# Four weight loads of a one-core kernel, each cut into a piece of 120 and a piece of 8 partitions

## What is computed

```
def peer_ffn(h, w_query, sub_keys, expert_u, expert_v):
    q = (ht @ w_query).reshape(T, Hh, 2, PEER_HALF)             # 1024 x 2048 matrix
    scores = einsum('thpd,hpkd->thpk', q, sub_keys)
    s_top, i_top = top_k(scores, 16)
    ...
    best, pos = top_k(cand, 16)                                  # 8 heads x 16 picks a token
    u = expert_u[idx]                                            # rows of 1024 floats
    a = gelu(einsum('tkd,td->tk', u, xb)) * g
    return einsum('tk,tkd->td', a, expert_v[idx])
```

## Time and profile before

| what | value |
|---|---|
| median of 3 runs | 2224.89 us (2223.32 to 2227.02) |
| span of the profiled execution | 2222.0 us |
| that execution's own time | not listed apart; the span is used |
| PE busy | 1963.9 us (88%) |
| DVE busy | 1560.3 us (70%) |
| ACT busy | 1033.6 us (47%) |
| POOL busy | 628.7 us (28%) |
| traffic, mean over the span | 761.24 MB, 343 GB/s |

### The profile page before, as it was taken

How to read it: one execution, slowest core, us unless ns; L and a number is a source line. 1 busy time by engine, 2 the same in 40 slices (tenths; PEclk the granted TensorE clock), 3 DMA queues, 4 the chain that set the end, 5 groups by cost and what they waited for, 6 DMA issues and landing times. The chain is left out here.

```text
span 2222.0 us, 24054 instructions
## 1 busy us (share of the span) xinstructions
PE 1963.9 (88%) x8090; PEld 1240.2 (56%) x8090; DVE 1560.3 (70%) x2943; ACT 1033.6 (47%) x2177; POOL 628.7 (28%) x552
## 2 busy tenths in 40 slices
PE   5999989987777888899999988888898889999998
PEld 5987845432222333479885544343343326888987
DVE  6987877676667775678878876676777755565554
ACT  4345545544444444444445644444455434544443
POOL 1000255544444444000014444444344430200000
PEclk9999999999999999999999999999999999999999
DMA  8897799999999999786589999999999995343553
GB/s 332 296 378 261 312 421 421 420 421 422 421 421 421 421 422 421 291 338 226 206 301 421 414 421 420 421 421 421 421 411 421 421 421 191 115 145 132 189 189 133
DMA packets 112396, 761.24 MB, mean 343 GB/s; under 512 B 12832, under 2 KB 13600, under 8 KB 26128
## 3 DMA queue, kind: packets, MB, share of 16 engines
q0 software_dynamic: 76480, 548.94, 59.7%
q1 hardware_dynamic: 34832, 207.74, 25.2%
q10 hardware_dynamic: 960, 3.01, 0.4%
HBM read 758.60 MB, written 1.05 MB: 342 GB/s over the span
## 5 line engine op out<-in xcount | busy, mean ns | idle before, releaser
L1046 PE MATMUL pair<-uv,p_diag 128*128 128x512 f32 x1352 | 653.2, 619 | 114.3 <-ACT p_diag L2374 112.4
L1743 DVE CUSTOM_DVE_ANT_0 uv<-uv,p_h 128x1024 f32<-128x1024 f32 x338 | 413.7, 1224 | 242.6 <-DMA uv<-in_peer_uv,p_idx 240.7
L573 POOL DMA_INDIRECT uv<-in_peer_uv,p_idx x338 | 398.3, 1179 | 522.8 <-PE pair L1046 385.9
L1046 PEld LDWEIGHTS pair<-uv,p_diag 128*128 128x128 f32 x1352 | 243.8, 193 | 493.5 <-ACT p_diag L2374 271.4
L1314 DVE TENSOR_TENSOR ring_low<-ring,ring_high 128x2048 fp32r<-128x2048 f32 x143 | 326.5, 2297 | 102.6 <-ACT ring_high L2156 101.4
L2366 ACT ACTIVATE p_act<-p_dot 128x1 f32<-128x1 f32 x512 | 103.5, 202 | 627.6 <-DVE p_dot L1743 625.5
L2156 ACT ACTIVATE ring_high<-ring 128x2048 fp32r<-128x2048 f32 x144 | 272.2, 1908 | 187.8 <-DMA ring<-in_ret_w_in 64.5
L725 PE MATMUL pair<-hT_high,ring_high 128*128 128x256 f32 x960 | 287.3, 299 | 0.2
L1046 PE MATMUL pair<-uv_high,p_diag 128*128 128x512 f32 x464 | 229.2, 625 | 52.5 <-ACT p_diag L2374 52.5
L725 PE MATMUL pair<-hT_low,ring_high 128*128 128x256 f32 x960 | 272.1, 283 | 0.0
L725 PE MATMUL pair<-hT_high,ring_low 128*128 128x256 f32 x896 | 254.1, 284 | 0.0
(11 more groups left out here) (413 smaller groups left out, 2660.1 us busy)
## 6 DMA issues: line engine op xcount, KB each, us to landing
ada<-in_ada_w SPq DMA_DIRECT2D x50, 512.0 KB, 5.9
ring<-in_ret_w_in SPq DMA_DIRECT2D x24, 1024.0 KB, 8.2
ring<-in_sgu_w_in SPq DMA_DIRECT2D x24, 1024.0 KB, 6.6
ring<-in_w_up SPq DMA_DIRECT2D x16, 1024.0 KB, 4.8
ring<-in_w_down SPq DMA_DIRECT2D x16, 1024.0 KB, 4.8
mod<-in_ada_w SPq DMA_DIRECT2D x30, 512.0 KB, 5.7
ring<-in_peer_w_query SPq DMA_DIRECT2D x12, 1024.0 KB, 8.5
ring<-in_sgu_w_out SPq DMA_DIRECT2D x12, 1024.0 KB, 4.9
```

What stands on the lines that cost most here:

```text
L573: nc.gpsimd.indirect_dma_start(uv_rows[SLOT[l][s]].rearrange("p a d -> p (a d)"), None, experts, bass.IndirectOffsetOnAxis(ap=p_idx[:, k:k ...
L1046: mm = nc.tensor.matmul(acc[:, half, :], p_diag[:, n % DIAGS, :], v[:, half * 512:(half + 1) * 512], start=(k == 0), stop=(k == PICKS - 1))
L1743: V.tensor_tensor_reduce(out=u, in0=u, in1=p_h[:, s // PICKS, :], scale=1.0, scalar=0.0, op0=ALU.mult, op1=ALU.add, accum_out=p_dot[:, n % ...
```

## The change

Blocks 6 and 7 of each of the two query matrices are no longer loaded by one DMA of 128 partitions but by two: partitions 0 to 119 and partitions 120 to 127, one after the other on SP's queue, into the same slot and with the same semaphore, each raising it by 16. `raw_count` counts two for such a block, so that all later waits on the slot's semaphore are for the matching value.

```diff
--- before.py
+++ after.py
@@ -63,6 +63,7 @@
 MEM_AT = (63, 69)
 MEM_NORM_AT = 22
 TILE_AT = (216, 224)
+MOST = 120
 
 
 TWO_PI_1 = 6.28125
@@ -226,7 +227,8 @@
         raw_at.append(early[i] if i in early else in_ring % R)
         in_ring += i not in early
     raw_before = [max((j for j in range(i) if raw_at[j] == raw_at[i]), default=None) for i in range(limit)]
-    raw_count = [sum(raw_at[j] == raw_at[i] for j in range(i + 1)) for i in range(limit)]
+    in_two = {query_first[l] + e for l in range(2) for e in (6, 7)}
+    raw_count = [sum(1 + (j in in_two) for j in range(i + 1) if raw_at[j] == raw_at[i]) for i in range(limit)]
     high_before = [max((j for j in range(i) if high_at[j] == high_at[i]), default=None) for i in range(limit)]
     low_by_pool = [0]
     low_by_dve = [i for i in range(limit) if i not in low_by_pool]
@@ -531,7 +533,11 @@
                         sp.wait_ge(h_ready, h_count(1 + 2 * l, 1, 1))
                 if i in behind_rows:
                     sp.wait_ge(dot_ready, behind_rows[i])
-                sp.dma_start(raws[raw_at[i]], blocks[i]).then_inc(w_in[raw_at[i]], 16)
+                if i in in_two:
+                    sp.dma_start(raws[raw_at[i]][0:MOST], blocks[i][0:MOST]).then_inc(w_in[raw_at[i]], 16)
+                    sp.dma_start(raws[raw_at[i]][MOST:P], blocks[i][MOST:P]).then_inc(w_in[raw_at[i]], 16)
+                else:
+                    sp.dma_start(raws[raw_at[i]], blocks[i]).then_inc(w_in[raw_at[i]], 16)
                 for j in loaded_after[i]:
                     if j == 6 * KD:
                         sp.wait_ge(x_ready, norm_count(2, 1))
```

## The result

The changed kernel takes 2242.99 us (median of 4 runs, 2241.67 to 2244.02), the kernel before 2224.11 in the runs beside it (2222.38 to 2227.02): ratio 1.0084, 95% interval 1.0072 to 1.0096. It is 18.9 us slower, far outside the range given.

A forecast was written before the change was run, and what follows sets the result against it. The prediction took the picks as bound by the DMA engines, the last to finish deciding. Gains of 1.6 to 2.2 us in layer 0 and 1.8 to 2.4 in layer 1, middle 4.0, gave 2224.9 - 4.0 = 2220.9 us; range 2217.5 to 2227.0.

The forecast's parts named there:

- A row costs 2.49 / 8 = 0.311 us of its engine: Picks and cut loads: a 128-row transfer takes 2.49 us with 8 rows per engine, so each row costs 0.311 us.
- the division that I assumed: Cut loads: 120 rows go to 15 engines, 8 each; the other 8 go to eight engines, 1 each.
- at worst: Cut loads: half of the engines carry the 120 rows, +2.5 us per block and +5.0 us per layer.
- the third: Rival on the cut loads: the 120 rows go to eight engines, the last among them; +5.0 us a layer, 2234.9; chance 0.07.
- the first case: End of each layer's picks: the relieved engine is the last to finish; gain 3.4 to 4.6 us, middle 4.0; chance 0.62.
- the light engine: Cut loads: the one engine given 16 rows fewer per layer, relieved of 5.0 us per layer.
- the lone step: End of layer 0's picks: DMA share 0.06, one engine alone about 2.2 us; short or gone if the forecast is right.
- Relief given early is kept: From the loads to the picks' end: engines work without a gap, so each finishes earlier by its relief, 5.0 us at most.
- SP's extra issues: SP's queue: two more issues per layer, 0.33 us each, covered by a wait for PE with 4.7 us left; cost 0.
- The consumers of block 6: ACT's turn of block 6: slack of 49 us in layer 0, about 50 in layer 1; cost 0.
- The rule that spoke against the change: Cut loads: two transfers to disjoint partition halves share the same engines, so by this rule the sum would be 0.

The follow-up runs named there:

- 112 + 16: Blocks 6 and 7 of each query matrix loaded as pieces of 112 and 16 partitions, against the kernel before: 2236.58 us, ratio 1.0054.
- 64 + 64: Blocks 6 and 7 of each query matrix loaded as two pieces of 64 partitions, against the kernel before: 2241.68 us, ratio 1.0075.
- the middle 64: Blocks 6 and 7 loaded in three pieces, partitions 32 to 95, 0 to 31 and 96 to 127, against the kernel before: 2232.91 us, ratio 1.0037.
- 96 + 32: Blocks 6 and 7 of each query matrix loaded as pieces of 96 and 32 partitions, against the kernel before: 2237.06 us, ratio 1.0058.
- The last experiment: Blocks 6 and 7 loaded as one piece of 64 partitions and eight pieces of 8, against the kernel before: 2262.39 us, ratio 1.0173.

## Why the prediction was wrong

**The step that failed** is "A row costs 2.49 / 8 = 0.311 us of its engine", carried from the loads of 128 partitions to pieces of other sizes. The packets agree with the division that I assumed (28 more for four blocks, 14 for two, 56 for eight), but in the cut loads a row is not served at that rate: the rate of all 16 engines fell from 421 to 248 GB/s for 21 us in layer 0, and the gathers that share the engines fell with it (4.69 to 2.74 MB in these 21 us). The sum priced a cut block at nothing for most engines; measured, it cost 3.6 to 4.7 us of all sixteen, where a whole block takes 2.49. My bound "at worst" (+5.0 us a layer) moved rows between engines and left their price alone, so it was no bound. The loss was 9.4 and 8.1 us in the two layers. None of my rivals held this mechanism; the third came nearest, at 2234.9 us, for another reason and with 0.07.

**Which partitions.** The runs say what makes a row dear: not having two pieces (by columns: nothing), not fewer than 16 engines (by their packets 112 + 16 and 64 + 64 run on 16), not the addresses read, and not the size of a piece alone (with the middle 64 the block costs half). The gathers aren't needed for it either, but beside them the price of a block is 2.4 to 2.9 times that in the MLP (4.7 us against 1.6 to 1.7, 4.2 against 1.5, 2.0 against 0.8). What fits is groups of partitions. The page "SBUF — State Buffer" of the Trainium skill, section "Door 1: The DMA port swizzle", describes them: 16 ports, four neighbouring partitions on one port, the same port again 32 partitions further on, and other ports for 64 to 127. "The descriptor swizzle" on the page "DMA: Bandwidth & Descriptors" adds that in a load of 128 partitions each engine has one port to itself. By that map a piece of 64 starting at 0 or 64 gives its 16 engines 8 ports, and 32 to 95 gives them 16; 15 engines with 8 neighbouring rows each would also be two to a port if they go in step. The measured order (64 + 64 16.7 us, three pieces 8.0, whole 0) and the landings (5.8 us, 4.5 us) agree. The ports themselves are seen in no row here; that each engine has neighbouring rows and that the engines go in step is inferred. The map doesn't give the sizes: if two engines on a port take turns, a block's 2.49 us would double (an estimate: 2.5 us more), but 64 + 64 cost 4.2 us beside gathers and 1.5 without them. Nor does it say by itself why 112 + 16 (11.6 us) and 96 + 32 (13.0) are cheaper than 64 + 64. And no run had one partial load in flight without the rest of its block, or issued the three pieces in another order.

**The gain of the first case** (the light engine is the last one, 0.62) did not come either: in layer 0 the last dot follows the last issue by 17.65 us as by 17.67 before, and the lone step is still there. (In layer 1 the prediction read the last engine as alone for 2.4 us; the share is 0.00 from 1841.0, so it was nearer 2.2.) Either the light engine is another one, or its relief was gone by then; no run tells these apart, and none shows what the change would bring without the clash.

**"Relief given early is kept"** was argued from a share of 1.01 in every window. The share is no proof of a rate, as 262 to 283 shows. The last experiment speaks against it only if its small pieces always go to the same eight engines, which no row shows: the 5 us that this would put between two halves of the engines were not there as such at the end.

**What held:** the picks are bound by DMA, and what is lost there goes through nearly one for one (8.6 + 8.0 us by the rates, 9.4 + 8.1 from the issue of block 6 to the last dot, 17.9 in the span). SP's extra issues cost nothing (four within 1.8 us, quicker than the 1.0 us spacing that I took, and 6.2 us of cover left). The consumers of block 6 had slack: its first use is at 331.59 in layer 0, 72 us after the issue. The cut by columns shows issues and waits together at no measurable cost. The rule that spoke against the change, in "Rules for kernel authors" on the page "DMA: Bandwidth & Descriptors" of the Trainium skill (one 128-partition transfer rather than two to disjoint halves of the partitions), gave the right advice. Its reason, that the parts share the same engines, would give 0 as the prediction read it; the runs show 2.0 us a block (three pieces) to 9.8 (nine pieces, 39.1 us for four blocks).

## What to carry to other kernels

Cut a load by columns, not by partitions: in two halves by columns a 1 MB load cost nothing here that the times can tell, in two parts by partitions beside gathers 2.9 to 4.7 us of all 16 DMA engines, whichever of the four cuts. Where DMA binds, that goes straight into the time; in the MLP, where PE was busy throughout, it did not show in the time, so a test in the wrong stage calls it free. Read the DMA share beside the GB/s: the share was 1.0 here at 421 GB/s and at 250, and only the second column told them apart. And look at the other queues: the gathers lost as much of their rate as the loads on SP's queue.

## What was not expected

With two blocks cut into 64 + 64 the mixed stretch ran at about 60% of its rate (254 GB/s against 421), though by the packets all 16 engines took part; with 64 partitions from 32 to 95 and two pieces of 32 it ran at 328. And the cut with the smallest pieces was the worst: one piece of 64 with eight of 8 brought the time to 2262.4 us, with 208 to 236 GB/s in the windows from 262 to 298.
